# A four-layer diffusion trunk on one core: the pool layer's modulation moved behind its pooling, and three modulation vectors moved into the first feed-forward

## The chip, the cores and the metric

One core of one Trainium2 chip. The metric is the device time of one execution in microseconds (us). One run's profile gives the trace that is read below. One core has a matrix engine (PE), a vector engine (DVE), a scalar engine (ACT), a general engine (POOL) and a queue engine (SP), which here only issues DMA transfers from memory. Engines wait for each other through semaphores, and each works its own list of instructions in order.

## The reference, cut to what matters

The model has four layers. Each has a token mixer (a pooling mixer in layer 0) and a feed-forward, and both are framed by normalisation and a modulation taken from a conditioning vector. There are 128 context tokens and 256 latent tokens, so two conditioning vectors.

```python
def modulation(cond, w, b):
    m = jax.nn.silu(cond) @ w + b
    return m.reshape(m.shape[:-1] + (N_MOD, D_MODEL))          # six vectors of 1024 for each layer

def modulate_in(x, mod, k, g):
    return rms_norm(x, g) * (1.0 + mod[:, None, 3 * k + 1]) + mod[:, None, 3 * k]

def gated_residual(x, out, mod, k, g):
    return x + mod[:, None, 3 * k + 2] * rms_norm(out, g)

def pool_mixer(h, w, scale):                # windows 2, 4, 8, 16, one for each quarter of the channels
    ...
        mean = (csg[:, hi] - csg[:, lo]) / (hi - lo).astype(jnp.float32)[None, :, None]
        outs.append(mean - hf[..., sl])
    p = jnp.stack(outs, axis=2).astype(h.dtype)
    y = jnp.einsum('blgc,gcd->blgd', p, w).reshape(h.shape)
    return y * scale

def ffn_sublayer(x, mod, g_pre, g_post, w_in, dw, dw_b, w_out):
    h = modulate_in(x, mod, 1, g_pre)
    return gated_residual(x, conv_ffn(h, w_in, dw, dw_b, w_out), mod, 1, g_post)
```

Pooling is linear in the tokens. With a matrix M of pooling weights, pooling `u * a + b` (u the normalised token, a and b one number for each channel) gives `a * (M u) + b * (row sums of M)`.

## The kernel before, in words

All 386 columns (128 context, a blank, 256 latent, a blank) go through the layers together. Products are made with split weights: ACT rounds a weight chunk of 128 by 1024 (`round_to`, `w_hi`, line 835), POOL and DVE each make half of the remainder (`low_to`, `w_lo`, lines 712 and 1186), and PE multiplies three times. SP loads chunks into four slots `raw` (`load_to`), and a slot is free once the remainders of its last chunk are made.

**Modulation vectors.** Each of the 24 vectors is made from four pieces of `w_mod`, 1 MB each. SP loads them into slots (`load_mod`), in its one list with all other loads. A piece waits for the last user of its slot. PE multiplies each (`mod_piece`, line 1664, 16 instructions in the trace), DVE turns and stores the vector (`mod_vector`) and makes coefficients (`coefficient`). Pieces 0 to 19 make the five *start vectors* of layer 0: vector 0 (SCALE0), 1 (SHIFT0), 2 (GATE0), 3 (SCALE1), 4 (SHIFT1). The start has seven slots. Pieces 20 to 31 make the next three vectors, GATE1 of layer 0 and SCALE0 and SHIFT0 of layer 1, which the end of layer 0 needs.

**The beginning** (`pool_mix` on PE). Pieces 0 to 7; the two coefficients are turned into rows (`turn_row`), stored to memory by ACT (`copy_row`) and loaded back spread over all partitions (`row0`); DVE makes the modulated tokens `h_rows` (lines 1611 and 1614); PE pools them in eight tiles of 128 channels (lines 2093 and 2097, banks 6 and 7 in turn); for each tile ACT rounds `h_hi` (line 1138) and DVE makes `h_lo` (line 1618). Pieces 8 to 11 make GATE0, which goes the way over memory too (`load_gate(0)` into `gb`). Then come the product with `pool_w` (lines 2116 to 2118) and the transition.

**The transition** takes three blocks of 128 tokens through, for each: `weigh` (lines 1240 and 1244, with `gb`), `residual` (1253), `unit` (1260), PE's turn (`turn_unit`, 1686), the modulated stage (ACT 876, DVE 1271), rounding `h_hi` (885) and the remainders (POOL 719, DVE 1279). In it PE makes pieces 20 to 31 (`fill`), and SP's list holds them ahead of most weight chunks.

**The first feed-forward** (`ffn_in(0)`) then makes 44 tiles, each 24 products of 386 columns (lines 1693 to 1695), each evacuated by ACT (922) and DVE (1310, 1317). The gate row of the feed-forward's own end is turned behind tile 3, copied by ACT behind its own evacuation of tile 3, and PE waits for that copy behind tile 4.

## Time and profile before

| | |
|---|---|
| time, median of 3 runs | 2098.58 us (2098.22 to 2098.79) |
| profiled execution: own time, span | 2101.43 us, 2099.7 us |
| mean granted TensorE clock | 0.964 of full |
| busy: PE, DVE, ACT, POOL | 1970.1, 1195.5, 919.6, 701.1 us |
| memory read | 319.34 MB, 155 GB/s over the span |

The span is the time from the first to the last instruction; the own time of the same execution also holds what lies around it. PE is busy for 94% of the span, but that is a mean over stretches with different limits: the first 128 us differ from the rest.

### The profile page before, as it was taken

The page shows a single profiled execution, that of the slowest core. Times are in us where ns is not written, and L with a number is a line of the kernel's source. Part 1 is how long each engine was busy: PE and PEld are TensorE (multiplying, and loading weights), DVE is VectorE, ACT ScalarE, POOL GpSimd, SP SyncE. Part 2 cuts the span into 40 slices and gives each one's busy share as a digit, 9 for nine tenths or more (in the row PEclk, how much of TensorE's full clock was granted, in tenths as well). Part 3 has the DMA queues.
Part 4 walks back from the last instruction along what each step waited for, and adds up shares of the span by engine and source line. Part 5 has one row for each costly group of instructions (what it writes and reads, how often), then busy time and mean ns, then how long its engine had stood idle before and what let it go on. Part 6 is the DMA issues. An engine that isn't in the chain of part 4 may idle for free.

```text
span 2099.7 us, 30072 instructions
## 1 busy us (share of the span) xinstructions
PE 1970.1 (94%) x11801; PEld 1744.9 (83%) x11801; DVE 1195.5 (57%) x1773; ACT 919.6 (44%) x1552; POOL 701.1 (33%) x515
## 2 busy tenths in 40 slices
PE   3779999999999989999999998899999969899998
PEld 1469998799998877799987865799987857799986
DVE  0567772366534565777733853777723674777722
ACT  1244442444545554544423424544424434544422
POOL 0033324233334445332243741323242321332342
PEclk6889999999999999999999999999999979999999
DMA  9954346544330135543454674444364413244442
GB/s 366 372 222 150 122 120 220 179 134 130 116 126 20 34 121 224 213 148 121 127 205 171 223 196 180 182 145 127 121 215 179 180 46 111 77 144 122 129 123 78
DMA packets 80667, 326.41 MB, mean 155 GB/s; under 512 B 9072, under 2 KB 17808, under 8 KB 66704
## 3 DMA queue, kind: packets, MB, share of 16 engines
q1 hardware_dynamic: 78928, 322.57, 44.5%
q8 instruction: 94, 1.54, 0.3%
q10 hardware_dynamic: 1600, 1.93, 0.3%
q14 instruction: 45, 0.37, 0.1%
HBM read 319.34 MB, written 5.12 MB: 155 GB/s over the span
## 4 chain that ended last, share of the span: by engine, by line
PE 82%; DVE 6%; ACT 4%; DMA 3%; issue 2%; POOL 1%; SPq 1%; DVEq 0%; ACTq 0%; POOLq 0%
PE pair L1693 17%; PE pair L1695 17%; PE pair L1694 17%; PE pair L1727 7%; PE pair L1728 6%; PE pair L1729 6%; PE pair L1841 3%; DMA mod_more<-in_w_mod 2%; DVE x L1253 2%; PE pair L1935 1%; ACT junk L863 1%; PE pair L1881 1%; PE pair L1846 1%; DMA ssd_cols<-in_ssd_cols 1%; DVE wk L1244 1%
## 5 line engine op out<-in xcount | busy, mean ns | idle before, releaser
L712 POOL TENSOR_TENSOR w_lo<-raw,w_hi 128x512 fp32r<-128x512 f32 (+1 forms) x375 | 574.7, 1534 | 1150.9 <-ACT w_hi L835 1150.7
L1693 PE MATMUL pair<-h_hi,w_hi 128*128 128x386 f32 (+1 forms) x2008 | 689.4, 343 | 18.8 <-POOL h_lo L719 16.2
L1695 PE MATMUL pair<-h_hi,w_lo 128*128 128x386 f32 (+1 forms) x2008 | 684.7, 341 | 0.0
L1694 PE MATMUL pair<-h_lo,w_hi 128*128 128x386 f32 (+1 forms) x2008 | 683.9, 341 | 0.0
L1186 DVE TENSOR_TENSOR w_lo<-raw,w_hi 128x512 fp32r<-128x512 f32 x351 | 430.6, 1230 | 317.1 <-ACT w_hi L835 317.0
L835 ACT ACTIVATE w_hi<-raw 128x1024 fp32r<-128x1024 f32 x375 | 392.8, 1050 | 285.3 <-PE pair L1729 224.5
L1693 PEld LDWEIGHTS pair<-h_hi,w_hi 128*128 128x128 f32 (+1 forms) x2008 | 381.8, 190 | 24.4 <-POOL h_lo L719 22.1
L1694 PEld LDWEIGHTS pair<-h_lo,w_hi 128*128 128x128 f32 (+1 forms) x2008 | 382.6, 191 | 0.9
L1695 PEld LDWEIGHTS pair<-h_hi,w_lo 128*128 128x128 f32 (+1 forms) x2008 | 381.7, 190 | 0.3
L1310 DVE SCALAR_TENSOR_TENSOR acc<-pair,taps,acc 128x385 f32<-128x385 f32 x176 | 108.8, 618 | 214.8 <-ACT acc L922 214.8
L922 ACT ACTIVATE acc<-pair,taps 128x386 f32<-128x386 f32 x176 | 117.4, 667 | 238.3 <-PE pair L1695 238.3
L1728 PE MATMUL pair<-w_hi,g 128*128 128x512 f32 x528 | 208.5, 395 | 0.0
L1729 PE MATMUL pair<-w_lo,g 128*128 128x512 f32 x528 | 208.4, 395 | 0.0
L1727 PE MATMUL pair<-w_hi,g 128*128 128x512 f32 x528 | 208.3, 395 | 0.0
L1727 PEld LDWEIGHTS pair<-w_hi,g 128*128 128x128 f32 x528 | 99.2, 188 | 23.4
L1728 PEld LDWEIGHTS pair<-w_hi,g 128*128 128x128 f32 x528 | 99.3, 188 | 23.3
L1729 PEld LDWEIGHTS pair<-w_lo,g 128*128 128x128 f32 x528 | 99.2, 188 | 23.3
L920 ACT ACTIVATE g<-gate 128x386 fp32r<-128x386 f32 x84 | 44.3, 527 | 162.4 <-DVE gate L1323 162.4
L1317 DVE SCALAR_TENSOR_TENSOR acc<-pair,taps,acc 128x385 f32<-128x385 f32 x176 | 108.5, 616 | 3.2
L991 ACT ACTIVATE mod_raw<-pair,shift 128x128 f32<-128x128 f32 x192 | 53.8, 375 | 32.0 <-PE pair L1846 31.9
L719 POOL TENSOR_TENSOR h_lo<-stage,h_hi 128x512 fp32r<-128x512 f32 x21 | 32.0, 1522 | 92.4 <-ACT h_hi L885 92.4
L1448 DVE TENSOR_TENSOR mod_raw<-mod_raw,pair 128x512 f32<-128x512 f32 x48 | 32.3, 685 | 53.3 <-ACT mod_raw L991 53.3
(277 smaller groups left out, 2195.6 us busy)
## 6 DMA issues: line engine op xcount, KB each, us to landing
raw<-in_ffn_in SPq DMA_DIRECT2D x176, 512.0 KB, 3.5
raw<-in_ffn_out SPq DMA_DIRECT2D x88, 512.0 KB, 3.6
mod_raw<-in_w_mod SPq DMA_DIRECT2D x32, 1024.0 KB, 7.5
mod_base<-in_w_mod SPq DMA_DIRECT2D x31, 1024.0 KB, 7.4
mod_more<-in_w_mod SPq DMA_DIRECT2D x20, 1024.0 KB, 13.7
raw<-in_ssd_conv SPq DMA_DIRECT2D x32, 512.0 KB, 3.5
gb<-rows_dram SPq DMA_DIRECT2D x8, 1024.0 KB, 5.2
raw<-in_ssd_z SPq DMA_DIRECT2D x16, 512.0 KB, 3.4
```

Of the source, the lines that this page charges most:

```text
L712: pool.tensor_tensor(w_lo[:, m % SLOTS, 0:w], raw[:, m % SLOTS, 0:w], w_hi[:, m % SLOTS, 0:w].bitcast(F32), ALU.subtract).then_inc(w_low_p ...
L835: act.activation(w_hi[:, m % SLOTS, 0:w], raw[:, m % SLOTS, 0:w], ACT.Copy).then_inc(w_rounded, 1)
L922: act.activation(acc[:, j % 4, :], tile_bank(j)[:, 0:COLS], ACT.Identity, scale=taps[:, l, j, 1:2], bias=taps[:, l, j, 3:4]).then_inc(acc_ ...
L1186: vec.tensor_tensor(w_lo[:, m % SLOTS, w0:w1], raw[:, m % SLOTS, w0:w1], w_hi[:, m % SLOTS, w0:w1].bitcast(F32), ALU.subtract).then_inc(w_ ...
L1310: vec.scalar_tensor_tensor(out=acc[:, j % 4, 1:COLS], in0=b[:, 0:COLS - 1], scalar=taps[:, l, j, 0:1], in1=acc[:, j % 4, 1:COLS], op0=ALU. ...
L1317: vec.scalar_tensor_tensor(out=acc[:, j % 4, 0:COLS - 1], in0=b[:, 1:COLS], scalar=taps[:, l, j, 2:3], in1=acc[:, j % 4, 0:COLS - 1], op0= ...
L1693: ten.matmul(to, wh, h_hi[:, k, cols], start=k == 0, stop=False, skip_group_check=True)
L1694: ten.matmul(to, wh, h_lo[:, k, cols], start=False, stop=False, skip_group_check=True)
L1695: ins = ten.matmul(to, wl, h_hi[:, k, cols], start=False, stop=k == KD - 1, skip_group_check=True)
L1727: ten.matmul(to, hi[:, k, cols], wh, start=first, stop=False)
L1728: ten.matmul(to, lo[:, k, cols], wh, start=False, stop=False)
L1729: ins = ten.matmul(to, hi[:, k, cols], wl, start=False, stop=last)
```

## The change: what it does

**Beginning.** `h_rows` becomes the normalised token alone (one DVE instruction for each block). PE multiplies the pooling matrices by ones (`pool_sums`). Behind each pooled tile ACT scales by the coefficient (two instructions, since context and latent columns have different numbers), DVE adds the shift times the sums (two instructions), ACT rounds and DVE makes the remainder from that result. The way of two rows over memory (`row0`) is gone. The first semaphore of loads covers four loads and no longer nine; the tables come later.

**Vectors 5 to 7.** Pieces 20 to 31 are no longer made in the transition but one behind each of tiles 2 to 13 of `ffn_in(0)`, through two slots. DVE makes their vectors at tiles 11 and 15, the gate row is turned behind tile 16, copied by ACT at tile 17, and PE waits for it behind tile 17. Pieces 12 to 19 move into the transition. Layer 0's first transition has an order of its own (`transition0`).

```diff
+INSIDE_SLOTS = 2
+INSIDE_FIRST = 2
...
-            s = i % (MOD_SLOTS if n else START_SLOTS)
+            s = i % (START_SLOTS if n == 0 else INSIDE_SLOTS if n == 1 else MOD_SLOTS)
...
-        LOADS0 = 16 * 9
+        LOADS0 = 16 * 4
...
+        def inside_piece(l, j):
+
+            i = j - INSIDE_FIRST
+            return end_pieces(0)[i] if l == 0 and 0 <= i < len(end_pieces(0)) else None
...
             sp.dma_start(pool_m[:, :, :], a["pool_m"]).then_inc(loaded0, 16)
...
+            load_mod(START_SLOTS)
+            load_to(2)
+            for p in range(START_SLOTS + 1, 3 * MOD_PIECES):
                 load_mod(p)
...
+            sp.dma_start(rowc[:, :], a["pool_scale"].broadcast_to([P, D])).then_inc(pool_scale_loaded, 16)
+            for p in range(3 * MOD_PIECES, 3 * MOD_PIECES + START_SLOTS):
                 load_mod(p)
             load_gate(0)
-            for p in range(16, MOD_PIECES * START_VECTORS):
+            for p in range(3 * MOD_PIECES + START_SLOTS, MOD_PIECES * START_VECTORS):
                 load_mod(p)
             load_to(4)
...
+                    if t == 1:
+                        for i in range(INSIDE_SLOTS, len(end_pieces(0))):
+                            load_to(s.n0 + INSIDE_FIRST + i + 2)
+                            load_ends(0, i)
+                        load_to(s.n0 + 24)
...
+            def transition0(n):
+                for c in range(3):
+                    first(0, c)
+                    second(0, c)
+                round_to(n + 2)
+                for c in range(3):
+                    unit_stage(0, c)
+                    unit_high(0, c)
+                act.wait_ge(tables_loaded, 64)
+                round_to(n + 4)
...
-                    if j == 3:
-                        copy_row(2 + 2 * l + 1)
+                    if j == (3 if l else 17):
+                        copy_row(2 * l + 1)
...
+            act.wait_ge(coef_ready, 1)
+            for k in range(KD + 1):
+                if k < KD:
+                    act.wait_ge(pooled, k + 1)
+                    if k >= 2:
+                        act.wait_ge(pooled_lo, k - 1)
+                    for s, cols in enumerate((slice(0, LAT0), slice(LAT0, COLS))):
+                        ins = act.activation(pooled_v[k % 2][:, cols], bank(6 + k % 2)[:, cols], ACT.Identity,
+                                             scale=coef[:, 0, 0, s, k:k + 1])
+                    ins.then_inc(pooled_scaled, 1)
+                if k:
+                    act.wait_ge(pooled_shifted, k)
+                    act.activation(h_hi[:, k - 1, :], pooled_v[(k - 1) % 2], ACT.Copy).then_inc(pooled_hi, 1)
             round_to(2)
-            copy_row(2)
...
+            def transition0(n):
+                for c in range(2):
+                    weigh(0, c)
+                    residual(0, c)
+                    unit(0, c)
+                mod_vector(3)
+                coefficient(0, 2)
+                weigh(0, 2)
+                residual(0, 2)
+                low_to(n + 2)
+                mod_vector(4)
+                vec.wait_ge(mod_done, START_VECTORS)
+                unit_stage(0, 0)
+                unit(0, 2)
+                unit_low(0, 0)
+                for c in (1, 2):
+                    unit_stage(0, c)
+                    unit_low(0, c)
...
+                    if l == 0 and j == 11:
+                        mod_vector(phases[1][0])
+                        mod_vector(phases[1][1])
+                    if l == 0 and j == 15:
+                        mod_vector(phases[1][2])
+                        coefficient(0, 3)
+                        coefficient(1, 0)
...
+            for k in range(KD + 1):
+                if k < KD:
+                    vec.wait_ge(pooled_scaled, k + 1)
+                    v = pooled_v[k % 2]
+                    for s, cols in enumerate((slice(0, LAT0), slice(LAT0, COLS))):
+                        ins = vec.scalar_tensor_tensor(out=v[:, cols], in0=pool_sums[:, k // 2, cols],
+                                                       scalar=modc[:, 0, SHIFT0, s, k:k + 1], in1=v[:, cols],
+                                                       op0=ALU.mult, op1=ALU.add)
...
+                if k:
+                    vec.wait_ge(pooled_hi, k)
+                    vec.tensor_tensor(h_lo[:, k - 1, :], pooled_v[(k - 1) % 2], h_hi[:, k - 1, :].bitcast(F32),
+                                      ALU.subtract).then_inc(pooled_lo, 1)
+            low_to(2)
+            mod_vector(2)
+            coefficient(0, 1)
...
-                if j == 3:
+                if j == (3 if t else 16):
                     turn_gate(t + 1)
-                if j == 4:
-                    ten.wait_ge(row_copied, 2 + t + 2)
+                if j == (4 if t else 17):
+                    ten.wait_ge(row_copied, t + 2)
...
                     in_tile(s, j, 2 * l)
+                    if inside_piece(l, j) is not None:
+                        mod_piece(inside_piece(l, j))
...
-                for p in range(3 * MOD_PIECES, START_VECTORS * MOD_PIECES):
+                for p in range(2 * MOD_PIECES, 3 * MOD_PIECES):
                     mod_piece(p)
+                turn_gate(0)
...
-                fill(0, 0, 3)
+                ten.wait_ge(weighed, event(0, 0) + 1)
+                for p in range(3 * MOD_PIECES, 4 * MOD_PIECES):
+                    mod_piece(p)
                 turn_unit(0, 0)
-                fill(0, 3, 7)
+                for p in range(4 * MOD_PIECES, START_VECTORS * MOD_PIECES):
+                    mod_piece(p)
```

PE's own loop over the eight pooled tiles keeps its wait: tile k from 2 on waits for the remainder `h_lo` of tile k - 2.

On ACT, in the pooling, this stands before the change (`h_hi<-pair` is the rounding of a pooled tile, `grow` a row on its way to memory, `std` the square root of the norm):

```order
L840 ACTIVATE std<-ssq,eps_col 128x1 [waits ssq_ready]
L908 ACTIVATE grow<-pair 16x128 [waits row_turned]
L910 DMA rows_dram<-grow 16x128 [waits row_copied]
...
L835 ACTIVATE w_hi<-raw 128x1024 [waits w_loaded0]
L835 ACTIVATE w_hi<-raw 128x1024 [waits w_loaded1]
...
L1138 ACTIVATE h_hi<-pair 128x386 [waits pooled] x8
L847 ACTIVATE junk,ssq<-wk 128x1024 [waits pre_ready]
```

And this stands there now (`stage<-pair,coef` is the scaling of a pooled tile, `h_hi<-stage` the rounding of the tile before it):

```order
L1164 ACTIVATE stage<-pair,coef 128x129 [waits pooled,coef_ready]
L1164 ACTIVATE stage<-pair,coef 128x257
L1164 ACTIVATE stage<-pair,coef 128x129 [waits pooled]
...
L1169 ACTIVATE h_hi<-stage 128x386 [waits pooled_shifted]
L1164 ACTIVATE stage<-pair,coef 128x129 [waits pooled_lo,pooled]
L1164 ACTIVATE stage<-pair,coef 128x257
L1169 ACTIVATE h_hi<-stage 128x386 [waits pooled_shifted]
```

The rounding of a tile has moved behind the scaling of the next tile, which waits for that next tile's pooling; the roundings of the weights and the gate's row have moved behind all eight tiles.

On SP, from the weights of the pool product to the second feed-forward chunks, this stands before the change (`mod_raw`, `mod_more` and `mod_row` are pieces, `gb` is the gate's row, `raw` a weight chunk):

```order
L551 DMA raw<-in_pool 128x1024 x2
L558 DMA gb<-rows_dram 128x2048 [waits row_stored0]
L542 DMA mod_more<-in_w_mod 128x2048 [waits mod_used] x4
L551 DMA raw<-in_ffn_in 128x1024 x2
L542 DMA mod_raw<-in_w_mod 128x2048 [waits mod_used] x2
L542 DMA mod_more<-in_w_mod 128x2048 [waits mod_used] x5
L542 DMA mod_row<-in_w_mod 128x2048 [waits rows_ready]
L542 DMA mod_row<-in_w_mod 128x2048
L551 DMA raw<-in_ffn_in 128x1024 [waits w_low_dve,w_low_pool] x2
```

And this stands there now:

```order
L586 DMA rowc<-in_pool_scale 128x1024
L554 DMA mod_more<-in_w_mod 128x2048 [waits mod_used] x2
L554 DMA mod_raw<-in_w_mod 128x2048 [waits mod_used] x2
L554 DMA mod_more<-in_w_mod 128x2048 [waits mod_used] x3
L570 DMA gb<-rows_dram 128x2048 [waits row_stored0]
L554 DMA mod_more<-in_w_mod 128x2048 [waits mod_used]
L563 DMA raw<-in_ffn_in 128x1024 x2
...
L554 DMA mod_raw<-in_w_mod 128x2048 [waits mod_used] x2
L563 DMA raw<-in_ffn_in 128x1024 [waits w_low_dve,w_low_pool] x4
L554 DMA mod_raw<-in_w_mod 128x2048 [waits mod_used]
L563 DMA raw<-in_ffn_in 128x1024 [waits w_low_dve,w_low_pool]
```

Seven pieces (12 to 18) now stand ahead of the gate's row, each behind the use of a slot; ten of the twelve pieces of vectors 5 to 7 alternate with single weight chunks, where they stood in one run before.

## Rows read from the trace of the kernel before

**Rows 1.** Windows: span; busy PE, PEld, DVE, ACT, POOL; clock; DMA share; GB/s.

```profile
88.26:128.39 40.13, 25.85 (x265) 15.49 (x263) 24.88 (x36) 19.82 (x37) 7.98 (x6) 0.81 0.81 335
128.39:318.18 189.79, 189.79 (x1058) 189.70 (x1059) 135.16 (x181) 88.86 (x130) 58.88 (x45) 0.99 0.43 136
```

**Rows 2.** Chain of work that ended last: start us, us, what.

```profile
96.67 23.20 DMA mod_more<-in_w_mod
```

**Rows 3.** Timeline of PE, pieces: start us, us, what, idle before.

```profile
13.65 1.57 PE L1664 MATMUL pair<-mod_more,cond 128*32 128x256 f32 x16 [1.39 <-DMA mod_more<-in_w_mod]
...
99.94 1.07 PE L1664 MATMUL pair<-mod_more,cond 128*32 128x256 f32 x16 [1.31 <-DMA mod_more<-in_w_mod]
...
104.93 1.93 PE L1664 MATMUL pair<-mod_more,cond 128*32 128x256 f32 x16 [0.94 <-DMA mod_more<-in_w_mod]
...
415.77 2.77 PE L1664 MATMUL pair<-mod_base,cond 128*32 128x256 f32 x48
```

**Rows 4.** Windows: clock while PE began the pooled tiles.

```profile
62.84:68.65 5.81, 5.80 (x16) 4.42 (x17) 2.88 (x4) 3.25 (x5) 3.45 (x2) 0.50 0.31 102
```

**Rows 5.** Timeline of all engines: the first pooled tile, and the fifth.

```profile
62.84 0.80 PE L2093 MATMUL pair<-pool_m,h_rows 128*128 128x129 f32 x2 [6.98 <-DVE h_rows L1614]
63.43 1.92 PE L2097 MATMUL pair<-pool_m,h_rows 128*128 128x257 f32 x4
...
70.60 0.49 PE L2093 MATMUL pair<-pool_m,h_rows 128*128 128x129 f32 x2
70.93 1.03 PE L2097 MATMUL pair<-pool_m,h_rows 128*128 128x257 f32 x4
71.08 0.56 DVE L1618 TENSOR_TENSOR h_lo<-pair,h_hi 128x386 fp32r<-128x386 f32 x1 [0.53 <-ACT h_hi L1138]
```

**Rows 6.** The page's costliest groups: count, busy us, mean ns, idle before.

```profile
L835 ACT ACTIVATE w_hi<-raw 128x1024 fp32r<-128x1024 f32 x375 | 392.8, 1050 | 285.3 <-PE pair L1729 224.5
...
L1310 DVE SCALAR_TENSOR_TENSOR acc<-pair,taps,acc 128x385 f32<-128x385 f32 x176 | 108.8, 618 | 214.8 <-ACT acc L922 214.8
L922 ACT ACTIVATE acc<-pair,taps 128x386 f32<-128x386 f32 x176 | 117.4, 667 | 238.3 <-PE pair L1695 238.3
```

**Rows 7.** Timeline of ACT and PE: four stage instructions; a turn at half clock.

```profile
99.38 1.49 ACT L876 ACTIVATE stage<-pair,modc,coef 128x128 f32<-128x128 f32 x4
...
106.80 1.97 PE L1686 MATMUL pair<-ident,wk 128*128 128x128 f32 x8
```

**Rows 8.** DMA issues from 60 to 80: count, KB each, median us to landing.

```profile
gb<-rows_dram SPq DMA_DIRECT2D x1, 1024.0 KB, 4.5
```

**Rows 9.** Timeline: one vector with its coefficient; the transition's first block.

```profile
79.25 0.45 DVE L1195 STREAM_TRANSPOSE mod_turned<-pair 128x256 f32<-128x256 f32 x1 [2.54 <-PE pair L1664]
...
79.95 0.17 DVE L1206 SCALAR_TENSOR_TENSOR coef<-modc,gains 128x16 f32<-128x16 f32 x1
...
88.26 1.22 DVE L1240 TENSOR_TENSOR wk<-pair,rowc 128x1024 f32<-128x1024 f32 x1 [2.35 <-PE pair L2118]
...
92.10 1.28 DVE L1253 SCALAR_TENSOR_TENSOR x<-wk,inv,x 128x1024 f32<-128x1024 f32 x1
...
94.60 0.30 ACT L840 ACTIVATE std<-ssq,eps_col 128x1 f32<-128x1 f32 x1
...
95.80 1.22 DVE L1240 TENSOR_TENSOR wk<-pair,rowc 128x1024 f32<-128x1024 f32 x1
```

**Rows 10.** Timeline of the transition's end.

```profile
123.63 1.36 DVE L1271 TENSOR_SCALAR stage<-pair,coef,modc 128x128 f32<-128x128 f32 x4 [6.39 <-PE pair L1686]
...
126.23 1.69 POOL L719 TENSOR_TENSOR h_lo<-stage,h_hi 128x512 fp32r<-128x512 f32 x1 [7.86 <-ACT h_hi L885]
...
128.39 0.66 PE L1693 MATMUL pair<-h_hi,w_hi 128*128 128x386 f32 x1 [4.79 <-POOL h_lo L719]
```

**Rows 11.** Timeline of the in-projection: ACT and DVE behind an odd tile.

```profile
173.60 0.67 ACT L922 ACTIVATE acc<-pair,taps 128x386 f32<-128x386 f32 x1 [2.43 <-PE pair L1695]
...
175.50 1.65 DVE L1186 TENSOR_TENSOR w_lo<-raw,w_hi 128x512 fp32r<-128x512 f32 x1
```

More of the change, by code:

```diff
@@ L281, in build_trunk @@
         log_dt = flat_wk[:, 704:896]
+        pool_sums = flat_wk[:, 0:len(WINDOWS) * COLS].rearrange("p (g n) -> p g n", g=len(WINDOWS))
+        pooled_v = [flat_stage[:, k * 512:k * 512 + COLS] for k in range(2)]
         x_end = by_dir(flat_wk[:, 1536:2048])
@@ L1601, in _ @@
             vec.wait_ge(consts, CONSTS)
+            for c in range(3):
+                invert(c)
+                vec.tensor_scalar(h_rows[:, c, :], x[:, c, :], inv[:, c:c + 1], None, ALU.mult).then_inc(rows_ready, 1)
+            vec.wait_ge(sums_made, 1)
+            for g in range(len(WINDOWS)):
+                ch.did(vec.tensor_copy(pool_sums[:, g, :], bank((0, 1, 2, 4)[g])[:, 0:COLS]))
             mod_vector(0)
@@ L1773, in free @@
                 def free(c):
+                    if l == 0 and c == 2:
+                        ten.wait_ge(mod_read, START_VECTORS + END_VECTORS)
                     if c < 2:
```

126 lines of the change are left out of this document (57 added, 69 removed).

## The prediction, made before the change was run

> **What bounds the kernel now.** I read the windows by stage first [rows 1]: the reader should see that the transition, 88.26 to 128.39, is not bound by PE, which works 25.9 of 40.1 us in it at a DMA share of 0.81. From 128.39 to 318.18, the first in-projection, PE is busy for all of 189.79 us at a DMA share of 0.43. So work that leaves the beginning can save time, and work put into the in-projection costs its full length. The chain [rows 2] names what the transition waits for: 23.20 us of loads of pieces. The whole question is therefore when the first in-projection product starts (128.39 now [rows 10]) and what is added behind it. From `ffn_out(0)` on nothing is changed in kind, and I cost it at nothing: the two pieces loaded later in SP's list are wanted only at that stage's end.
>
> **The new beginning.** Pieces land 2.5 us apart when DMA runs without a gap (99.94 and 104.93 are two apart [rows 3]). Piece 3 starts on PE at 13.65. Behind it now come x, gains, b_mod, three pieces and pool_m: 2982 KB and 3072 KB, 14.6 us at that rate, so the four loads are there at about 29, counting some 0.8 for the small rows.
>
> PE then multiplies four matrices by ones, 2.5 us each at half clock, 1.4 at full (62.84 to 65.35, 70.60 to 71.96 [rows 5]). Half clock lasted 5.8 us of dense work before [rows 4], so I take 7.5 us, until 36.5. Pieces 4 to 7 in a dense row are 2.77/3 = 0.92 each at full clock [rows 3]: the first pooled tile starts at 40.3. The norms, sum copies and two vectors run beside this. Tiles 0 and 1 follow each other; tile 2 waits for the remainder of tile 0 and starts at about 45.0.
>
> **From there the loop is serial.** Tile k + 1 waits for the remainder of k - 1, which stands on DVE behind the shift of k, which needs ACT's scaling of k, which needs PE's tile k. Prices: scaling is two instructions from PSUM of 129 and 257 columns; 128 columns take 0.37 [rows 7] and 386 take 0.67 [rows 6], between them 0.87 for both. The shift is two of 0.30 and 0.45 by the 385-column row of 0.618 [rows 6]; bounds for the two together are 0.62 and 1.24. ACT's rounding, below its 0.67 for as many columns, lies beside the shift. The remainder is 0.56 [rows 5], four hand-overs 0.05 each. With PE's 1.36 at full clock the period is 3.7 us, with 2.51 at half 4.8.
>
> Which clock? In this loop PE works 1.36 us and then waits 2.3. The nearest rows are pieces in the transition, each of 1.07 us with gaps of about 1.3 between them: two pieces later the same piece took 1.93, which is the lower of the two clock levels (1.2 and 2.4 GHz) [rows 3]. I take full clock for tile 2 and half from tile 3. Tile 7 then ends at 45.0 + 3.7 + 4 x 4.8 + 2.5 = 70.4; before, the eight tiles took 14 us.
>
> **What waits behind the loop.** Piece 8 follows on PE and is used at 70.4 + 1.9 = 72.3. Only then does SP's list move: piece 15 waits for piece 8's slot, 16 to 18 for the next three, and the gate's row stands behind them. The row by itself landed 4.5 us after its issue [rows 8]; the same for piece 15, then four more of 2.5 each: 72.3 + 4.5 + 10 = 86.8. The chain through GATE0 itself (piece 11 at 77.5, coefficient, turn, copy, store, 4.5) would end near 86 and is no later. So `weigh` of the first block starts at S = 86.8, against 88.26 now [rows 9].
>
> **The new transition.** Two blocks at 7.54 each (88.26 to 95.80 [rows 9]): 15.1. Vector 3 with its coefficient, 79.25 to 80.12 [rows 9], 0.9: 16.0. Third block to its residual, 88.26 to 93.38: 21.1. Square and root, to 94.90: 22.6. Two roundings on ACT (1.05 each [rows 6]) and DVE's half of the second remainder (0.7 to 1.65, the upper end in [rows 11]; I take 1.1), together 3.2: 25.8. Vector 4, 0.7: 26.5. ACT's stage 1.5: 28.0. Turn of block 1 at half clock 2.0 [rows 7], DVE stage 1.4 [rows 10], turn of block 2, stage: 34.8. Meanwhile POOL has a remainder of block 1 (1.7 [rows 10]), one of a weight chunk and one of block 2, one behind the other from 32.5: 37.6. PE starts 0.5 later: 38.0. The transition took 40.1 with its 23.2 us of loads, so the order without waits is almost as long: all its blocks are now in series. First in-projection product: 86.8 + 38.0 = 124.8, a gain of 3.6.
>
> **Inside the in-projection.** Twelve pieces at 0.92: 11.1 us (bounds 0.87 and 1.07 each, 10.4 and 12.8), none hidden, since PE has no gap there. DMA has room: 1.5 MB in each 5.2 us. Each piece has two tiles and a piece, 9.4 us, from the release of its slot to its use, against 4.5 to land; a weight chunk behind it is late by some 6 us and is wanted ten later. The gate row: ACT copies it behind the evacuation of tile 17 (0.67 [rows 6], and about half as much for the row's 128 columns, 0.3 to 0.37 [rows 7]), while PE already waits: 1.0. At tile 16 the coefficient comes behind DVE's work on tile 15 (3.6 us after its evacuation begins [rows 11], then 0.9), against a tile of 4.25: 0.4. Together 1.4. The old wait behind tile 4 cost nothing.
>
> **Sum:** -3.6 + 11.1 + 1.4 = +8.9 us. The profiled execution would go from 2101.43 (span 2099.7 and 1.7 around it) to 2110.3; it stands 2.85 above the median of the runs. On the median: 2098.58 + 8.9 = 2107.5 us. A difference under 0.2%, 4.2 us, can't be told from none.
>
> **Rivals.**
> Full clock in the loop. The pieces fell to half clock, but they are other instructions than pooled tiles. At 3.7 us throughout, tile 7 ends at 64.7, piece 8 at 65.6, S = 80.0, in-projection at 118.0: -10.4 + 11.1 + 1.4 = +2.1, 2100.7. The Trainium skill, "TensorE: Matmul & The Clock Gate", on the clock gate, says the clock falls back once PE has been idle for a while; the gaps here are 2.3 us at most and the page would let them pass. The pieces ahead of 104.93 had shorter gaps and the clock fell, so the trace does not agree. Chance 0.17.
>
> The loop overlaps (faster). If scaling, shift and remainder of two neighbouring tiles overlap as the two bank copies allow, the old rhythm of 14 us holds: tile 7 ends at 54.3, piece 8 at 55.2, S = 69.6, in-projection at 107.6: -20.8 + 12.5 = -8.3, 2090.3. It decides from a period below about 2.7 us for tiles 2 to 7 (S = 76.6 breaks even). For it: the old loop. Against it: the order of ACT's and DVE's lists, which ties each remainder to the next tile's pooling. Chance 0.12.
>
> Pieces starve the in-projection. If a piece with its chunk takes 12 us to land and not 4.5 to 7, each of ten pieces is 2.6 late on half of the tiles: +13 on top, 2120. Against it: the DMA share of 0.43. Chance 0.07.
>
> **Chances and range.** The forecast as worked out has the rest, 0.64; its own range is 2103 (loop partly at full clock, short pieces) to 2113 (shift at 1.24, pieces at 1.07, sums at half clock). The full-clock case lies within 0.2%. Of the likeliest case I count a little as within 0.2%, and of the overlap case nearly all as faster. Faster 0.12, same 0.19, slower 0.69. The range for 8 in 10 takes in the full-clock case: 2098 to 2114, a little beyond both.
>
> **What would show it.** The four loads near 29; the eight pooled tiles over 30 us, with their period at 4.8 and PEclk at 0.50; SP issuing the gate's row behind four pieces at about 80; `weigh` at 87 and not before 80; first in-projection product near 125; twelve pieces of 0.9 to 1.1 us between tiles, without PE gaps; one gap of about 1 us behind tile 17. A period under 3 us, a `weigh` before 77, or pieces that wait for DMA would make the prediction wrong.

## The result, and the profile after

The changed kernel takes 2113.42 us (median of 6 runs, 2111.66 to 2115.37). The kernel before, run beside it, takes 2099.95 (6 runs). The ratio is 1.0064, with an interval of 1.0054 to 1.0075: the change costs about 13.5 us. The forecast was 2107.5, within 2098 to 2114. The direction is as predicted and the size is 4.6 us short. Between the two profiled executions the span grows from 2099.7 to 2113.6 us, by 13.9.

The windows of the changed kernel by stage: the pooled loop, the way to the first `weigh`, the transition, the first in-projection (columns as in [rows 1]).

```profile
38.17:66.98 28.81, 16.32 (x53) 10.84 (x56) 8.70 (x22) 7.62 (x20) 0.00 (x0) 0.62 0.45 190
66.98:87.24 20.26, 13.57 (x137) 10.76 (x137) 5.19 (x9) 3.83 (x7) 3.45 (x2) 0.92 0.68 260
87.24:125.68 38.44, 14.77 (x153) 8.81 (x153) 24.72 (x41) 20.14 (x37) 8.52 (x6) 0.63 0.47 175
125.68:331.00 205.32, 204.37 (x1250) 193.73 (x1251) 131.66 (x181) 89.30 (x130) 63.63 (x45) 0.99 0.52 178
```

The reader should see two things. The transition is still 38 us long although DMA is now at 0.47 in it (0.81 before [rows 1]): the loads are gone from it and the time is not. And the in-projection, without PE gaps before, is 205 us long and still nearly without gaps.

One turn of the pooled loop, in the timeline of all engines. Scaling on ACT, shift and remainder on DVE, then PE's next tile, which had waited 2.08 us:

```profile
50.67 0.80 PE L2172 MATMUL pair<-pool_m,h_rows 128*128 128x129 f32 x2 [2.08 <-DVE h_lo L1687]
...
51.27 1.92 PE L2176 MATMUL pair<-pool_m,h_rows 128*128 128x257 f32 x4
53.22 0.73 ACT L1164 ACTIVATE stage<-pair,coef 128x129 f32<-128x129 f32 x2 [3.45 <-PE pair L2176]
...
53.99 0.75 DVE L1678 SCALAR_TENSOR_TENSOR stage<-wk,modc,stage 128x129 f32<-128x129 f32 x2 [3.37 <-ACT stage L1164]
54.66 0.55 DVE L1687 TENSOR_TENSOR h_lo<-stage,h_hi 128x386 fp32r<-128x386 f32 x1
...
55.27 0.80 PE L2172 MATMUL pair<-pool_m,h_rows 128*128 128x129 f32 x2 [2.08 <-DVE h_lo L1687]
```

Tile 2 (at 42.64) still ran at full clock; from tile 3 on the granted clock is 0.50 (third number from the end):

```profile
46.08:66.98 20.90, 12.58 (x34) 8.12 (x38) 4.88 (x12) 4.58 (x12) 0.00 (x0) 0.50 0.24 102
```

The chain that ended last, from the loop to the in-projection and on (start, length, what). First the gate row's way over memory, then the end of the transition, then two pieces between tiles, two plain tiles far behind, and the first product of `ffn_out(0)`:

```profile
74.46 4.96 DMA rows_dram<-grow
79.44 7.72 DMA gb<-rows_dram
...
87.24 1.24 DVE wk L1272
...
125.68 0.66 PE pair L1762
...
140.83 1.00 PE pair L1733 x16
...
146.28 1.00 PE pair L1733 x16
...
225.15 0.18 PE pair L1764
...
314.47 0.18 PE pair L1764
...
331.12 0.23 PE pair L1798
```

From one piece to the next are 5.45 us. Between 225.15 and 314.47 lie 21 tiles of 4.253 us each. So a piece costs **1.20 us**, not its 1.00. PE's timeline around the first piece shows where the rest is: products start 0.18 us apart, but 0.27 lie ahead of the piece (140.49 to 140.76) and 0.28 behind the first product after it (141.76 to 142.04), which is 0.09 and 0.10 more.

```profile
140.32 0.34 PE L1763 MATMUL pair<-h_lo,w_hi 128*128 128x386 f32 x1
140.49 0.34 PE L1764 MATMUL pair<-h_hi,w_lo 128*128 128x386 f32 x1
140.76 1.07 PE L1733 MATMUL pair<-mod_raw,cond 128*32 128x256 f32 x16
141.76 0.45 PE L1762 MATMUL pair<-h_hi,w_hi 128*128 128x386 f32 x1
142.04 0.34 PE L1763 MATMUL pair<-h_lo,w_hi 128*128 128x386 f32 x1
...
220.29 0.44 PE L1762 MATMUL pair<-h_hi,w_hi 128*128 128x386 f32 x1 [0.91 <-ACT grow L933]
```

**Where the 13.9 us are.** The first in-projection product starts at 125.68 instead of 128.39 [rows 10]: -2.7. The in-projection takes 331.12 - 125.68 = 205.44 instead of 189.79 [rows 1]: +15.65, of which twelve pieces are 14.4 and the gate row 1.2 (0.91 of wait, the rest its turn). Behind 331.12 the kernel takes 1782.5 us, before 1781.5: +1.0. This can't be told from chance: in the profiles of the changed kernel and of the eleven runs below, which are the same program there, the span behind the first product of `ffn_out(0)` lies between 1779.7 and 1785.4 us.

### The profile page after: what moved, and what is told of

Its sections match the earlier page's. It is cut to its first block, busy times and chain, and to the rows that moved or that the text cites. A ratio compares the mean times of both kernels' runs of the same rounds, so it can differ in the third digit from the quotient of the medians.

```text
span 2113.6 us, 30143 instructions
## 1 busy us (share of the span) xinstructions
PE 1975.8 (93%) x11823; PEld 1750.3 (83%) x11823; DVE 1193.5 (56%) x1790; ACT 924.7 (44%) x1566; POOL 705.9 (33%) x515
## 4 chain that ended last, share of the span: by engine, by line
PE 83%; DVE 7%; ACT 5%; issue 2%; DMA 2%; POOL 1%; SPq 0%; DVEq 0%; ACTq 0%; POOLq 0%
PE pair L1762 17%; PE pair L1764 17%; PE pair L1763 17%; PE pair L1798 7%; PE pair L1799 6%; PE pair L1800 6%; PE pair L1916 3%; DVE x L1285 2%; PE pair L2010 1%; ACT junk L877 1%; DMA pool_m<-in_pool_m 1%; PE pair L1733 1%; DVE wk L1276 1%; PE pair L1921 1%; PE pair L1956 1%
## 5 line engine op out<-in xcount | busy, mean ns | idle before, releaser
L1219 DVE TENSOR_TENSOR w_lo<-raw,w_hi 128x512 fp32r<-128x512 f32 x351 | 422.8, 1207 | 343.9 <-ACT w_hi L849 343.8
```

Source lines behind the costliest of these rows:

```text
L1219: vec.tensor_tensor(w_lo[:, m % SLOTS, w0:w1], raw[:, m % SLOTS, w0:w1], w_hi[:, m % SLOTS, w0:w1].bitcast(F32), ALU.subtract).then_inc(w_ ...
```

## The experiments

All runs in one table, by the profile of each: start of the first `weigh`, of the first in-projection product and of the first product of `ffn_out(0)`, in us, then the median and the ratio to the kernel before with its interval. Runs under one line in italics shared a chip with runs of the kernel before, whose median there was 2100.07, 2100.69 and 2101.84; the ratios are against these. A, B, C and D below are the theories and rivals of the text printed ahead of each result. The first three columns of a row come from one profile. The three kernels *changed*, *one product* and *pairs* are the same program up to the in-projection, and their first `weigh` starts at 87.2, 86.6 and 84.9: a difference of 2 us in this column can be chance.

| kernel | weigh | in-projection | ffn_out(0) | median | ratio |
|---|---|---|---|---|---|
| before | 88.3 | 128.4 | 318.0 | 2099.95 | 1 |
| changed | 87.2 | 125.7 | 331.0 | 2113.42 | 1.0064 (1.0054 to 1.0075) |
| *runs 1 to 4* | | | | | |
| one product of eight | 86.6 | 125.1 | 324.4 | 2106.77 | 1.0033 (1.0021 to 1.0045) |
| pairs | 84.9 | 123.4 | 332.1 | 2118.07 | 1.0082 (1.0068 to 1.0096) |
| old start, pieces inside | 87.3 | 120.9 | 325.7 | 2109.81 | 1.0044 (1.0031 to 1.0057) |
| pieces 8 to 11 in the loop | 75.8 | 114.3 | 320.0 | 2102.84 | 1.0008 (0.9999 to 1.0017) |
| *runs 5 to 8* | | | | | |
| four buffers | 65.8 | 104.3 | 310.1 | 2094.36 | 0.9965 (0.9953 to 0.9977) |
| four buffers, pieces in the loop | 67.7 | 106.2 | 310.8 | 2093.53 | 0.9962 (0.9948 to 0.9976) |
| and transition interleaved | 67.7 | 103.4 | 309.2 | 2088.76 | 0.9943 (0.9930 to 0.9956) |
| and weights early, turn late | 66.8 | 102.4 | 305.4 | 2088.77 | 0.9939 (0.9925 to 0.9952) |
| *runs 9 to 11* | | | | | |
| changed, row ahead | 80.3 | 118.9 | 324.2 | 2109.01 | 1.0036 (1.0023 to 1.0049) |
| all, row ahead | 61.7 | 98.1 | 302.3 | 2085.00 | 0.9916 (0.9902 to 0.9929) |
| all, row ahead, pairs | 63.6 | 98.9 | 299.9 | 2083.88 | 0.9914 (0.9900 to 0.9928) |

### 1. What a piece costs inside

This kernel makes one product of the eight of a piece inside and leaves out seven, in `mod_piece` as the in-projection calls it:

```diff
                 for k in range(2):
                     for q in range(4):
+                        if products and (k, q) not in products:
+                            continue
...
-                        mod_piece(inside_piece(l, j))
+                        mod_piece(inside_piece(l, j), [(1, 3)])
```

> The changed kernel with only one of the eight products of each of the twelve pieces inside the in-projection (vectors 5 to 7 are left wrong; all loads, waits and evacuations stay). In the changed kernel the in-projection repeats every 5.455 us where a piece stands behind a tile, against 24 products of 0.177 = 4.25 us without: 1.20 us for a piece whose own row is 1.00. Theory A (a piece costs its products, 1.0 us, and about 0.2 us more because the weights of 32 columns and of 128 columns follow each other with a gap at either end): one product in eight leaves about 0.2 to 0.25 of work and the 0.2 of the seam, period 4.7 us, twelve times 0.75 less: 2104.4 us, a ratio to the kernel before of 1.002. Theory B (the piece is mostly a stop of PE at the seam, whatever it multiplies): period above 5.2 us, time above 2110. Theory C (the in-projection is held by loads of pieces and chunks behind each other): the loads are the same, so the period stays at 5.45 and the time at 2113.

PE's timeline of this kernel, around two such pieces:

```profile
139.53 0.62 PE L1735 MATMUL pair<-mod_raw,cond 128*32 128x256 f32 x2
140.08 0.45 PE L1764 MATMUL pair<-h_hi,w_hi 128*128 128x386 f32 x1
...
144.54 0.62 PE L1735 MATMUL pair<-mod_raw,cond 128*32 128x256 f32 x2
145.09 0.45 PE L1764 MATMUL pair<-h_hi,w_hi 128*128 128x386 f32 x1
```

The period is 5.01 us, so a piece with an eighth of its products still costs 0.75. The time lies between A (2104.4) and B (above 2110): an eighth of the products leaves three fifths of the price. The loads were the same and the period fell, so C falls.

The pairs put a number on the seam, which is the time lost at the two ends of each visit of PE to the pieces:

```diff
-                    if inside_piece(l, j) is not None:
-                        mod_piece(inside_piece(l, j))
+                    if j % 2 and inside_piece(l, j) is not None:
+                        mod_piece(inside_piece(l, j - 1))
+                        mod_piece(inside_piece(l, j))
```

> The changed kernel with the twelve pieces in six pairs, behind tiles 3, 5, ... 13 instead of one behind each of tiles 2 to 13; the same work. Theory A (0.2 us for each seam): six seams fewer, 12 tiles with their pieces take 1.2 us less (64.2 instead of 65.4 us), time 2112.2 us, ratio 1.006. Theory B (the price stands in the piece itself): a pair costs 2.4 us, time 2113.4. Rival D: two pieces and two chunks, 3 MB, must land in the 10.7 us between two pairs, which is about what DMA moves at its best; if they don't, PE waits at each pair and the time is 2115 to 2125, with PE waits for loads in the trace.

The chain of this kernel: two pairs, then the load of a chunk that stood behind two pieces, and the gate row's coefficient and turn.

```profile
142.31 1.86 PE pair L1733 x32
...
152.85 1.86 PE pair L1733 x32
...
186.92 9.69 DMA raw<-in_ffn_in
...
213.14 0.18 DVE coef L1242
213.36 0.38 PE pair L1741
```

The same turn in PE's timeline, with its wait:

```profile
213.36 0.38 PE L1741 MATMUL pair<-ident,coef 128*16 128x128 f32 x1 [3.56 <-DVE coef L1242]
```

And a window of it right behind the turn (clock, third number from the end):

```profile
213.30:219.30 6.00, 5.94 (x19) 5.94 (x20) 3.37 (x7) 2.03 (x3) 1.27 (x1) 0.50 0.37 127
```

Two tiles and a pair take 10.54 us, so a pair costs 10.54 - 8.51 = 2.03. With one piece at 1.20, the second of a pair costs 0.83 and the seam, once for each visit, **0.37**. That is A with a larger seam than the 0.2 that I gave it, and six seams fewer gain 2.2 us. All the same the kernel is slower: the late chunk delays ACT's rounding, that DVE's evacuations, that the coefficient, and PE stands 3.6 us at the turn; the next 6.0 us then run at a clock of 0.50 and cost 3.0 us more. Rival D named late loads, but PE waited for none of them: it was a queue of three engines behind one load that ended in the turn.

With this seam the run before fits too, though 0.75 less 0.37 is far more than an eighth of 0.83. A piece's 16 instructions take 0.83 us, 0.05 each, while pooled products of the same form on all 128 columns start 0.22 apart (four of them in the 0.87 from 43.02 to 43.89 in the run with four buffers, section 3): the pieces' instructions run four side by side. The two that are left in that run have no neighbours. By an estimate from these rows they take 0.43 us, half of the piece, and 0.75 - 0.43 leaves 0.32 for the seam. So A's 0.2 to 0.25 for the one product was too little as well.

One rival of the seam can be looked up: the pieces and the tiles around them also differ in the number format (f32 against fp32r). In the run with four buffers the pooled tiles are f32 like the pieces, and the ends look the same. The last four products, from 46.30, take 0.87, and the piece behind them starts 0.09 us later than that, at 47.26. Behind the piece ahead of the first tile, that tile's two groups of products start 0.33 apart (38.32 and 38.65), in the next tiles 0.22. So the format is not what makes the seam.

The Trainium skill, "TensorEngine Tiling (Array Packing)", Tiling Modes, says that a change of the tiling mode drains the engine. The pieces are products of 32 columns each (128*32 in the rows), the tiles of 128, and the seam agrees with it; that the drain is all of the 0.37 us no run here shows.

### 2. Which half of the change costs what

The other half alone: the kernel before with its own beginning, and only vectors 5 to 7 and the second gate row moved.

```diff
-                fill(0, 0, 3)
+                ten.wait_ge(weighed, event(0, 0) + 1)
                 turn_unit(0, 0)
-                fill(0, 3, 7)
                 turn_unit(0, 1)
-                fill(0, 7, None)
                 turn_unit(0, 2)
...
                     in_tile(s, j, 2 * l)
+                    if inside_piece(l, j) is not None:
+                        mod_piece(inside_piece(l, j))
```

> The kernel before with its own beginning, and only the other half of the change: vectors 5 to 7 made inside the first in-projection, the gate row turned at tile 16. Theory A (the rebuilt beginning is itself slower than the old one once the twelve loads are gone from it, because its loop is serial and its gate row stands behind four pieces): the old transition starts at 88.3 as before, and without the 23.20 us of loads its DVE and ACT work alone carries it, 88.3 to about 119.5; then 15.7 us for what is inside. 2099.95 - 8.9 + 15.7 = 2106.7 us, ratio 1.0032, well below the changed kernel's 2113.4. Rival B (the transition's length is its own work, near 38 us as in the changed kernel): first in-projection product at 126.5, time 2113.8, ratio 1.0066, so that the two beginnings are worth the same.

A came nearer: 2109.81, ratio 1.0044; its interval takes in A's 1.0032 and not B's 1.0066. The transition begins at 87.3 and hands over at 120.9, 33.6 us later (expected 31). So with the twelve loads gone the in-projection starts 7.5 us earlier behind the old beginning, and only 2.7 earlier behind the new one. Grouped rows of its trace: `weigh`'s first instruction, three times, and the in-projection's first line, with the first and the last start:

```profile
L1253 DVE TENSOR_TENSOR wk<-pair,rowc x3: 1218/1219/1224, 87.3 to 103.9; 128x1024 f32<-128x1024 f32 x3
```

```profile
L1714 PE MATMUL pair<-h_hi,w_hi x352: 336/340/660, 120.9 to 325.2; 128*128 128x386 f32 x176
```

### 3. The loop and the gate row

The changed kernel with pieces 8 to 11 in the loop's waiting time, and the gate row made there:

```diff
                     ins.then_inc(pooled, 1)
-                for p in range(2 * MOD_PIECES, 3 * MOD_PIECES):
-                    mod_piece(p)
-                turn_gate(0)
+                    if 1 <= k <= MOD_PIECES:
+                        mod_piece(2 * MOD_PIECES + k - 1)
+                    if k == 6:
+                        turn_gate(0)
...
+                if k == 5:
+                    mod_vector(2)
+                    coefficient(0, 1)
...
+                if k == 7:
+                    copy_row(0)
```

> The changed kernel with pieces 8 to 11 multiplied behind the pooled tiles 1 to 4 of the serial loop (in PE's waiting time) instead of behind the loop, so that their slots come free early, GATE0's coefficient is made and its row turned, copied and stored inside the loop, and SP's issue of the gate row no longer stands behind four pieces at the loop's end. Theory A (the weigh of the first block, at 87.24 in the changed kernel, is set by the gate row, and its 4.96 us store and 7.72 us load are long because pieces 15 to 18 are under way then): the row is there before 70, weigh starts when the pool product's first block is done, near 77; first in-projection product 10 us earlier, 2103.2 us, ratio 1.0015. The loop keeps or shortens its period of 4.59 us, since the pieces fill PE's gaps. Rival B (the pieces stand in the loop's chain): period 4.59 + 1 to 2 us for four tiles, loop end 4 to 8 us later, gain 2 to 6 us: 2107 to 2111. Rival C (weigh waits for something else just behind the gate row): gain below 2 us.

2102.84, and `weigh` at 75.8: A. PE's timeline of this loop:

```profile
45.93 0.49 PE L2174 MATMUL pair<-pool_m,h_rows 128*128 128x129 f32 x2 [1.08 <-DVE h_lo L1688]
46.25 1.03 PE L2178 MATMUL pair<-pool_m,h_rows 128*128 128x257 f32 x4
47.22 1.07 PE L1735 MATMUL pair<-mod_more,cond 128*32 128x256 f32 x16
49.37 0.49 PE L2174 MATMUL pair<-pool_m,h_rows 128*128 128x129 f32 x2 [1.08 <-DVE h_lo L1688]
...
56.24 0.80 PE L2174 MATMUL pair<-pool_m,h_rows 128*128 128x129 f32 x2 [2.08 <-DVE h_lo L1688]
```

The window of the tiles with pieces behind them (clock, third number from the end):

```profile
42.49:54.16 11.67, 8.43 (x72) 4.85 (x72) 3.66 (x9) 3.44 (x9) 0.00 (x0) 1.00 1.02 423
```

With a piece between the tiles the gap is 1.08 us, the granted clock stays at 1.00 and the period is 3.44. Behind the last piece the gap is 2.08 again and the tile at 56.24 runs at half clock, as all tiles from 46.08 on in the changed kernel. The pieces cost the loop nothing. They shorten the gap and lengthen PE's work between gaps at once, so which of the two holds the clock is not shown.

Is the gate row's lateness the order of SP's list? One line moved in the changed kernel:

```diff
-            for p in range(3 * MOD_PIECES, 3 * MOD_PIECES + START_SLOTS):
+            for p in range(3 * MOD_PIECES, 15):
                 load_mod(p)
             load_gate(0)
-            for p in range(3 * MOD_PIECES + START_SLOTS, MOD_PIECES * START_VECTORS):
+            for p in range(15, MOD_PIECES * START_VECTORS):
```

> The changed kernel with one line of SP's list moved: the gate row is issued ahead of pieces 15 to 18 instead of behind them. Theory A (the 4.96 us of the small store and the 7.72 us of the row, 74.46 to 87.24 in the changed kernel, are those four pieces in the queue ahead of them; with the queue empty the store took about 1.4 and the row about 4.5 us in the kernel before): store there at 75.9, row at 80.5, weigh of the first block at 80.5 to 81, 6.5 us earlier. The four pieces come later instead, behind the row, and are used 15 to 25 us behind weigh, so that nothing else waits for them: 2106.9 us, ratio 1.0033. Rival B (the pieces are late then): the stage of the first block waits for vector 4, gain of 0 to 3 us, time 2110 to 2113. Rival C (the store's 4.96 us is its own): weigh at 84 or later.

The chain of that kernel:

```profile
74.43 1.42 DMA rows_dram<-grow
75.87 4.35 DMA gb<-rows_dram
```

The store takes 1.42 instead of 4.96 and the row 4.35 instead of 7.72: A. The store is clear: in the three profiles of the old order (changed, one product, pairs) it took 4.77 to 5.13. The row took 7.72, 6.63 and 5.26 in the same three, so a part of its 3.4 us is chance. `weigh` starts at 80.3, 6.9 us earlier than in the changed kernel and 4.6 to 6.9 earlier than in the three, and the in-projection as much; the ratio, 1.0036, is close to A's 1.0033. That much of the row's lateness was the four pieces ahead of it; the kernel with the pieces in the loop, with `weigh` at 75.8, shows that its place behind the loop costs at least 4.5 more.

And the loop's rhythm, by four buffers for the pooled tiles in the changed kernel:

```diff
-        pooled_v = [flat_stage[:, k * 512:k * 512 + COLS] for k in range(2)]
+        pooled_v = [flat_stage[:, k * 512:k * 512 + COLS] for k in range(4)]
...
+        def pooled_bank(k):
+            return bank((6, 7, 0, 1)[k % 4])
...
-                    if k >= 2:
-                        ten.wait_ge(pooled_lo, k - 1)
+                    if k == 2:
+                        ten.wait_ge(dve, len(WINDOWS))
+                    if k >= 4:
+                        ten.wait_ge(pooled_scaled, k - 3)
```

> The changed kernel with four buffers for the pooled tiles instead of two (banks 6, 7, 0 and 1, four quarters of the staging tile), so that a tile no longer waits for the remainder of the tile two before it; nothing else is moved. Theory A (the loop's 4.59 us a tile is the chain scaling, shift, remainder and a product at half clock behind each other, because of two buffers; the gate row follows the loop's end by 20.3 us, 66.9 to 87.24): the loop takes some 14 us as in the kernel before, ends near 52 instead of 67, the weigh of the first block starts at 72.5, the time is 14.7 us less: 2098.7 us, ratio 0.9993. Rival B (the loads set the gate row by then: pieces 12 to 18 and the row go behind each other whatever the loop does): weigh at 78 to 80, time 2104 to 2106. Rival C (the order of ACT's and DVE's lists ties the tiles, not the buffers): the period stays above 3.5 us, time above 2106.

PE's timeline, two neighbouring tiles of the eight, and the end of the last one with the piece behind it:

```profile
42.80 0.38 PE L2177 MATMUL pair<-pool_m,h_rows 128*128 128x129 f32 x2
43.02 1.03 PE L2181 MATMUL pair<-pool_m,h_rows 128*128 128x257 f32 x4
43.89 0.39 PE L2177 MATMUL pair<-pool_m,h_rows 128*128 128x129 f32 x2
44.11 1.03 PE L2181 MATMUL pair<-pool_m,h_rows 128*128 128x257 f32 x4
...
46.30 1.03 PE L2181 MATMUL pair<-pool_m,h_rows 128*128 128x257 f32 x4
47.26 1.07 PE L1736 MATMUL pair<-mod_raw,cond 128*32 128x256 f32 x16
```

A, and more: the period is 1.09 us with no gap and at full clock, the loop ends near 47 instead of 67, and `weigh` starts at 65.8 instead of the 72.5 that I gave A. B and C fall. With this one edit the rebuilt beginning wins: 2094.36. The edit changes two things at once, though: there are four buffers, and PE waits for a tile's scaling and no longer for its remainder, which comes two steps later in the chain. A run with two buffers and the earlier release is missing, so how much of the 3.5 us of period each of them is worth is not shown.

Four buffers and the pieces in the loop together, by the two edits shown:

> Four buffers for the pooled tiles and, as in the run before with the pieces in the loop, pieces 8 to 11 behind tiles 1 to 4 with the gate row stored inside the loop. Theory A (with both, neither loop nor gate row holds the first block; the pool product does, which starts its weigh 10.2 us behind the loop's end as it did there): the pieces are no longer in waiting time and add 1 us each, loop end near 56.5, weigh at 67, first in-projection product at 105.4, 20.3 us earlier than in the changed kernel: 2093.1 us, ratio 0.9967. Rival B (the loads hold it: the pieces of the loop or the pool product's weights come late): weigh at 72 or later, time above 2098.

The stages came as A said (`weigh` at 67.7, in-projection at 106.2, 2093.53), but they are no gain over four buffers alone: their intervals overlap. A loop without gaps has no waiting time for the pieces; they lengthen it, and so the early row is worth nothing there.

### 4. The transition, and what is left

Vector 3 ahead of the pool product, and the blocks interleaved as in the kernel before:

```diff
-            return bank((5, 3, 5, 0, 1)[i])[:, 0:MOD_BANK_COLS]
+            return bank((5, 3, 5, 3, 1)[i])[:, 0:MOD_BANK_COLS]
...
+                for p in range(3 * MOD_PIECES, 4 * MOD_PIECES):
+                    mod_piece(p)
                 chunk_ready(0)
                 chunk_ready(1)
...
+            mod_vector(3)
+            coefficient(0, 2)
-            transition0(lin["ffn_in0"].n0)
+            transition(0, lin["ffn_in0"].n0)
```

> The run with four buffers and the early gate row, and the first transition in the order of the kernel before (the blocks interleaved), with vector 3 made ahead of the pool product in bank 3 and vector 4 behind the first block. Theory A (38.4 us from weigh to the first in-projection product is the price of the blocks in series; the old order takes 33.6, as it did with the old beginning and the pieces inside): 4.8 us less than the run without it, 2088.3 us, ratio 0.9944. Rival B (vector 3 ahead of the pool product makes that wait for its pieces): weigh 3 to 6 us later, nothing gained. Rival C (vector 4 is late for the first block's stage): gain of 1 to 3 us.

`weigh` to the first product takes 35.7 us instead of 38.5: 2.8 of A's 4.8, and the size that C gave, with `weigh` where it was. This step can be trusted to a few tenths, since in the seven profiles with the blocks in series it takes 38.4 to 38.6. The medians are 4.8 apart, more than this step explains. The chain shows what is left:

```profile
81.34 0.37 DVE mod_turned L1223
...
82.03 1.50 ACT stage L893 x4
83.53 1.04 ACT junk L880 x2
```

Vector 4 and the first block's stage now stand ahead of the second block's square, 2.2 us which the chain with the old beginning doesn't have there (its square starts at 100.93, right behind the residual). Vector 4's pieces were done on PE at 77.3, so it is late by its place in DVE's list and not by its loads. Series against interleaving is about 3 us.

To that, weights ahead and the second gate row later:

```diff
+            round_to(2)
             act.wait_ge(coef_ready, 1)
...
-                if j == (3 if t else 16):
+                if j == (3 if t else 18):
                     turn_gate(t + 1)
-                if j == (4 if t else 17):
+                if j == (4 if t else 24):
```

> The run before, and in addition the pool product's weights rounded and their remainders made ahead of and inside the pooled loop, and the second gate's row turned behind tile 18 of the in-projection with ACT's copy behind tile 20 and PE's wait at tile 24. Theory A: the pool product starts behind the four pieces of vector 3 instead of behind POOL's remainders, about 3 us earlier, and the in-projection loses its 0.9 us wait: 2084.4 us, ratio 0.9926. Rival B (the product was held by pieces 12 to 15): only 0.9 to 1.5 us less than the run before. Rival C (SP's list stands longer at the second gate row and the chunks come late): a new wait in the in-projection, no gain.

Not told apart from the run before by the time: 2088.77. PE's wait in the in-projection is gone and `ffn_out(0)` starts 3.8 us earlier. Of these, 1.6 are chance as far as the edit goes: PE reached full clock 3.0 us into the in-projection, and in the run before 6.1. The profiled execution then takes 3.3 us longer behind `ffn_out(0)`, which the edit doesn't touch, within the spread of that stretch. At the front `weigh` gained 0.9 only; the row held it:

```profile
66.76 1.23 DVE L1267 TENSOR_TENSOR wk<-pair,rowc 128x1024 f32<-128x1024 f32 x1 [7.04 <-DMA gb<-rows_dram]
```

The row ahead of pieces 16 to 18 in this kernel, by the same line of SP's list with 16 for 15:

> The last kernel of the series before (four buffers, pieces 8 to 11 in the loop, interleaved transition, weights early, late turn) with the gate row issued ahead of pieces 16 to 18. There DVE waited until 66.76 for the row, stored from 56.54 and issued at 61.08. Theory A: store 1.4 us, row 4.5 us behind it, weigh at 63 (the pool product's first block is there at about 62.5), 3.8 us earlier; the pieces of vector 4 land by 73 and are wanted at 76: 2085.0 us, ratio 0.9923. Rival B (vector 4 is late for the first block's stage): weigh at 63, but the first in-projection product stays within 1 us of 102.4: 2088.

2085.00, A's time; the interval of the ratio overlaps that of the run before, so it is the stages that show the gain: `weigh` starts at 61.7 and the in-projection 4.3 us earlier. B falls. The chain now goes through a piece of vector 4, so the next limit is near:

```profile
59.12 13.78 DMA mod_more<-in_w_mod
```

The pairs once more, in this kernel:

> The run before with the pieces in pairs behind every second tile, as in the earlier run with pairs, where a pair took 2.03 us against 2 x 1.20, but a chunk behind two pieces landed 9.69 us after its issue, ACT's rounding and DVE's evacuations came late through it, and the turn at tile 16 waited 3.6 us for its coefficient, after which PE ran at half clock until 219. Here the turn stands at tile 18, 8.5 us later. Theory A (those 3.6 us and the half clock behind them were what the pairs lost): without them the pairs gain their twelve times 0.18 us: 2.2 us less than the run before, 2082.8 us. Rival B (the late chunk itself costs PE time, whatever is turned when): equal or up to 3 us more than the run before, with PE waiting for a chunk's remainder or an evacuation in the in-projection.

The chain shows the same 10.54 us from pair to pair, and no wait at the turn:

```profile
117.60 1.86 PE pair L1717 x32
128.14 1.86 PE pair L1717 x32
```

By the stages this is A. The in-projection takes 201.0 instead of 204.2 us in the two profiles: 2.2 us are the pairs; the rest is that PE reached full clock sooner in its first 12 us (granted clock 0.86 instead of 0.77). 2083.88 against 2085.00 can't be told apart by the runs. This version and the one before it are the fastest of the study, 17 to 18 us below the kernel before.

## Why the prediction was right, and where it was short

**Right.** The four loads were there at 28.47, for about 29. The pooled tiles ran in a serial loop, tile 2 at full clock and the others from tile 3 at half, with a period of 4.59 for 4.8. `weigh` started at 87.24, for 86.8, with the gate's row behind four pieces. Section 3 undoes the loop and the row's place one at a time, and `weigh` comes earlier each time. The transition ran its blocks in series and took 38.4 us, for 38.0. The pieces ran without PE gaps, with one gap of 0.91 behind tile 17.

**In part luck: the 87.24.** The loop ended at 66.98 and not at 70.4: its first tile began 2.1 us early, since loads and sums took less, and the period was shorter. From there to `weigh` the kernel took 20.3 us and not 16.4. The prediction let SP's list set the row (piece 8's slot, then four pieces and the row); in the trace SP had issued those pieces by 72.0 and then waited for the store, which ended GATE0's own chain at 79.42. The prediction had that chain end near 86, no later than the list, and counted no delay for the store; the store took 4.96 us, and the row 7.72 and not 4.5. The two errors, 3.4 us early and 3.9 late, nearly cancel. The row's 7.72 is itself the longest of three profiles of the same beginning.

**Short: "Twelve pieces at 0.92".** The sum was -3.6 + 11.1 + 1.4 = +8.9; measured are -2.7 + 14.4 + 1.2, and 1.0 behind, together 13.9. The step that was mis-sized is the piece inside: 1.20, also outside the bounds of 0.87 and 1.07. The price came from a dense row of pieces (2.77 for three [rows 3]), and a dense row has no seam. The runs give 0.83 for the products and 0.37 for the seam. The other differences are within chance: the in-projection of the three kernels with the same beginning starts at 125.7, 125.1 and 123.4, around the predicted 124.8, and the 1.0 behind is within the spread of that stretch.

**Two slips in the working.** The terms of the half-clock period as priced (0.87, 0.75, 0.56, 0.20 and 2.51) add to 4.89 and not 4.8. And the start of `weigh` at which the change breaks even is 86.8 - 8.9 = 77.9 by the prediction's own sum and not 76.6. With a piece at 1.20 it lies lower: the run with `weigh` at 75.8 took 2102.84, ratio 1.0008.

**The rivals.** *Full clock in the loop* did not happen: behind gaps of 2.08 us the granted clock fell to 0.50, the lower level, from tile 3 on. The Trainium skill, "TensorE: Matmul & The Clock Gate", on the clock gate, says that the clock falls back once PE has been idle for a while, and the prediction read from it that such gaps would pass; the trace does not agree. With a piece in each gap, gaps of 1.08 us, the clock held at 1.00. *The loop overlaps* did not happen in the changed kernel; with four buffers and the earlier release it did, at a period of 1.09, and its verdict, faster than before, was right for a kernel with that edit. *Pieces starve the in-projection* did not happen with single pieces; in pairs a late load reached PE, by way of the turn.

**What stays open.** No run shows what in the seam is drain and what is the load of the first weights, which part of the loop's period is the second pair of buffers and which the earlier release, or why PE reached full clock between 3.0 and 6.1 us into the in-projection.

## What to carry to other kernels

A work item that is moved into a dense stage can cost more than its own length, as the pieces did by a seam of 0.37 us at each visit. Read its price as the longer period of that stage, not from rows in which such items follow each other, and try moving them in groups. A loop across three engines runs at the sum of its chain when each tile waits for the last step of the tile two before it, and here PE, idle in between, fell to half clock on top; ask what a buffer really has to wait for, and count buffers against the steps of the chain, before such a loop replaces one that works. Try a small store, and the row read back after it, ahead of bulk loads: here the store took 1.42 us instead of 4.96. And before explaining a microsecond in one stretch of a trace, look at how much that stretch differs between profiles of programs that are the same there.

## What the runs showed of the hardware that was not expected

- Switching PE from products with 128 columns of weights to four side by side with 32, and back, cost 0.37 us for each visit (0.32 by the estimate from the run with one product).
- Tiles of 1.36 us with gaps of 2.08 fell to half clock at the second such gap (46.08). With a piece behind each tile and gaps of 1.08 the clock stayed at 1.00, and the first gap of 2.08 after that was followed by half clock (56.24).
- A single wait of 3.6 us in a dense stretch was followed by 6.0 us at a granted clock of 0.50.
- An 8 KB store took 4.77 to 5.13 us to land in three profiles with four 1 MB loads ahead of it, and 1.42 without them, though it was issued from another engine's queue.
